# How often the mixer's weight matmuls let other TensorE work in: every 512 contracted rows in place of every 128

## The reference

```python
proj = h @ w_in + b_in                      # 14 groups of columns, the last one 5 x 1024 gates
y_a  = gated delta rule on chunks (l2 norms, triangular solve, scan over the state)
y_b  = causal convolution of 31 taps, layer norm
y_c  = sliding-window attention with sinks, blocks of 128 queries
y_d  = real-gated linear recurrence
y_e  = cross-attention to 256 memory rows
branch_out = einsum('bsnw,nwd->bsnd', [y_a .. y_e], w_br)
merged = sum(sigmoid(gates) * branch_out, axis=branches)
x = x + rms_norm(merged @ w_out)
```

## Time and profile before

| | us |
|---|---|
| three runs | 3691.21, 3688.09, 3692.55 |
| median | 3691.21 |
| the profiled execution | 3682.18 |
| its span, first to last instruction | 3680.3 |

### The profile page before, as it was taken

The page is one execution under the profiler, slowest core; times in us unless marked ns, Lnnn a source line. Parts: engine busy times, 40 slices in busy tenths (PEclk is TensorE's granted clock), DMA queues, the critical chain, the costliest instruction groups (busy, mean ns, idle before and its releaser), DMA issues. The chain is left out here.

```text
span 3680.3 us, 36134 instructions
## 1 busy us (share of the span) xinstructions
PE 3182.3 (86%) x14755; PEld 2462.0 (67%) x14755; DVE 1413.8 (38%) x1628; ACT 1037.5 (28%) x1428; POOL 619.2 (17%) x287
## 2 busy tenths in 40 slices
PE   1976988866499999995599999995999999999995
PEld 1864444425388888884477777774777788888874
DVE  4003333331341414133646777664754122232223
ACT  2113433331211111112246332321333432232222
POOL 1201111012222222220212100001111122222220
PEclk8987999987799999998799999997999999999997
DMA  2213000011011111111223111113333412212121
GB/s 98 91 58 114 18 18 0 1 46 46 19 49 47 51 47 46 51 46 53 105 88 121 52 64 49 50 55 76 114 99 113 177 49 95 92 65 78 52 92 51
DMA packets 105272, 242.61 MB, mean 66 GB/s; under 512 B 7464, under 2 KB 53160, under 8 KB 104872
## 3 DMA queue, kind: packets, MB, share of 16 engines
q1 hardware_dynamic: 96632, 209.65, 16.9%
q10 hardware_dynamic: 8496, 30.94, 2.1%
HBM read 182.89 MB, written 57.67 MB: 65 GB/s over the span
## 5 line engine op out<-in xcount | busy, mean ns | idle before, releaser
L1624 PE MATMUL psum<-normed_hi,w_hi 128*128 128x512 f32 x1632 | 674.7, 413 | 42.6 <-POOL w_lo L2166 37.3
L1626 PE MATMUL psum<-normed_hi,w_lo 128*128 128x512 f32 x1632 | 639.8, 392 | 0.0
L1625 PE MATMUL psum<-normed_lo,w_hi 128*128 128x512 f32 x1632 | 639.1, 392 | 0.0
L2166 POOL TENSOR_TENSOR w_lo<-buffer,w_hi 128x1024 fp32r<-128x1024 f32 x122 | 309.9, 2540 | 1526.5 <-ACT w_hi L1200 1526.5
L1624 PEld LDWEIGHTS psum<-normed_hi,w_hi 128*128 128x128 f32 x1632 | 309.2, 189 | 114.6 <-POOL w_lo L2166 38.8
L1626 PEld LDWEIGHTS psum<-normed_hi,w_lo 128*128 128x128 f32 x1632 | 308.1, 189 | 66.3
L1625 PEld LDWEIGHTS psum<-normed_lo,w_hi 128*128 128x128 f32 x1632 | 309.2, 189 | 63.5 <-issue 7.7
L1200 ACT ACTIVATE buffer<-psum,par 128x512 f32<-128x512 f32 (+1 forms) x196 | 138.0, 705 | 528.2 <-PE psum L1626 513.4
L556 POOL TENSOR_TENSOR w_lo<-buffer,w_hi 128x1024 fp32r<-128x1024 f32 x64 | 156.0, 2438 | 531.6 <-ACT w_hi L590 531.6
L516 PE MATMUL psum<-normed_hi,w_hi 128*128 128x512 f32 x512 | 200.1, 391 | 33.1 <-POOL w_lo L556 33.1
L517 PE MATMUL psum<-normed_lo,w_hi 128*128 128x512 f32 x512 | 199.8, 390 | 0.0
(11 more groups left out here) (318 smaller groups left out, 5320.3 us busy)
## 6 DMA issues: line engine op xcount, KB each, us to landing
buffer<-in_w_in SPq DMA_DIRECT2D x67, 512.0 KB, 4.1
buffer<-in_w_mlp SPq DMA_DIRECT2D x64, 512.0 KB, 3.3
scratch_in<-buffer ACTq DMA_DIRECT2D x59, 512.0 KB, 2.6
buffer<-in_w_gate SPq DMA_DIRECT2D x40, 512.0 KB, 3.4
buffer<-scratch_in SPq DMA_DIRECT2D x32, 512.0 KB, 7.1
buffer<-scratch_y SPq DMA_DIRECT2D x20, 512.0 KB, 7.5
buffer<-in_w_br SPq DMA_DIRECT2D x20, 512.0 KB, 3.3
res<-in_x SPq DMA_DIRECT2D x2, 4096.0 KB, 14.3
```

What stands on the lines that cost most here:

```text
L1624: pe.matmul(out, hi, xh, start=k == 0, stop=False)
L1625: pe.matmul(out, hi, xl, start=False, stop=False)
L1626: mm = pe.matmul(out, lo, xh, start=False, stop=k == unit.kc - 1)
L2166: pool.tensor_tensor(ws.lo[:, n % 2], raw[:, n % 2], ws.hi[:, n % 2].bitcast(F32), ALU.subtract).then_inc(w_lo, 1)
```

## The change

The `gemm` lane on TensorE yields its due time at contraction steps 0 and 4 of a unit only. Four steps (twelve matmuls) in a row can no longer be divided by another lane. A unit of eight steps has two places where other work can enter in place of eight, and a `br` unit one in place of four.

```diff
                     for k in range(unit.kc):
-                        yield pace(n + k / unit.kc)
+                        if k % 4 == 0:
+                            yield pace(n + k / unit.kc)
                         if k == 0:
```

## The result

| | median, us | runs, us |
|---|---|---|
| before | 3689.65 | 3686.48 to 3692.55 |
| changed | 3713.09 | 3710.61 to 3715.89 |

The changed kernel is slower by 23 us, ratio 1.0064 with a 95% interval of 1.0046 to 1.0081. The forecast was 3724 us with a range of 3702 to 3752 us. The profiled execution of the changed kernel took 3714.68 us (span 3712.6 us) and lies close to its median. That of before (3682.18 us) lay 7.5 us under its own: it reached the mixer's first weight matmul at 1792.68 us, the changed one at 1800.94 us, though the program is the same up to there. So the two traces are compared by the length of their stages, not by their spans.

A forecast was written before the change was run, and what follows sets the result against it. In-order TensorE was taken to bound the delta-rule stage, so waits add to the end. Their sums rise from 39.2 to 71.8 us, +32.6 us on the 3691.2 us median: 3724 us, range 3702 to 3752 us.

The forecast's parts named there:

- L1735 to L1742: Delta-rule stage, levels 1 to 5: L1742 directly behind L1735 in 23 levels; TensorE waits 7.5 us before, 22.5 us after.
- L1735 to L1746, level 6: Delta-rule stage: trip of 3.2 us behind ScalarE's exponentials, adjacent in five chunks; waits 9.3 us before, 10.5 us after.
- L1746 and L1725 to the next L1735: Delta-rule stage, two kinds of wait: behind L1746 7.5 us before, 16.8 after; behind L1725 9.0 before, 10.5 after.
- L1704 to L1710: Delta-rule stage: three covering steps gone in three chunks, 1.55 us each; waits 0.8 us before, 4.7 us after.
- L1712 to L1725: Delta-rule stage: one of the two smaller kinds of wait, 4.6 us before and 4.3 us after.
- the first L1692: Delta-rule stage: one of the two smaller kinds of wait, 0.5 us before and 2.5 us after.
- rival c: Delta-rule stage: waits make the clock fall, ten waits of over 2 us cost 20 us, 3744 us; chance 8%.
- rival b: Between delta-rule and window stages: the 41.7 us idle at L1825 swallow the delay, no change, 3691 us; chance 6%.
- rival a: Delta-rule stage: longer batches pay, with fewer changes of work and shrinking trips; faster, about 3680 us; chance 5%.
- Fewer runs: First step behind a small block: each vanished run returns 0.01 us, at the other bound 8 us in all; taken as nothing.
- The window stage: Eight steps between scores and transposes in both orders, so no cost; at most 0.9 us in some eight windows, 7 us.
- The check on the method: Trace of before: waits of some 28 us plus 9 us of matmul tails, together 37 us, against the summed 39.2 us.

## Why the prediction was right, and where its sizes were off

**TensorE is the bound and lost cover is added to the end.** Right. 25.7 of the stage's 27.6 us are idle time of TensorE, and the groups of four in this stage alone reproduce the loss.

**L1735 to L1742.** Right in mechanism and count: 23 adjacent levels, 23 waits. The remainder of time between blocks, taken from the starts in both traces, was 10.3 us at L1742 before and is 21.4 us after (forecast 7.5 and 22.5). Before was sized too small: a block behind even a short wait takes 0.1 us longer (L1742 to L1746 is 2245.31 - 2244.32 = 0.99 us in the earlier trace rows, against 0.89 us), which the formula left out.

**L1735 to L1746, level 6.** All remainders ahead of L1746, with the 0.1 us behind L1742 in the other levels, went from 10.8 to 11.0 us. Of level 6 itself the view of waits shows 6.7 us in both kernels, six waits before and five after; with the tails of the five, 7.5 us stand where 10.5 were forecast. The adjacent trips came to 2.0 to 2.9 us; they too shrank, and only two of the five waits are over 1.5 us.

**L1746 and L1725 to the next L1735.** This is the term that was mis-sized most. Together 18.4 us became 22.4 us, where 16.5 and 27.3 us stood. The trips were taken as fixed, and some are not. Where VectorE had a convolution step or GpSimd's split beside the mask, the trip shrinks when TensorE comes later: L1725 to L1735 in the first chunk is 3.34 us in the changed kernel and was 4.73 us, in the second 4.69 and was 5.60 us, and the 4.3 us behind L1746 in the seventh is 3.4 us. The prediction had 12 us of shrinking trips in its lower bound; here 5 of them came, and 3 in level 6.

**L1704 to L1710, L1712 to L1725, the first L1692.** 0.9 to 5.0, 4.3 to 4.7 and 2.2 to 4.2 us, near the forecast differences (+3.9, -0.3, +2.0).

**The clock (rival c).** The forecast gave it 8% as what decides; it came as a small part. The changed kernel has four stretches in this stage with the clock well under 1.00, before there was one. Two of them, and TensorE in the second:

```profile
2075.00:2090.00 15.00, 10.35 (x53) 9.17 (x53) 9.35 (x11) 1.31 (x3) 0.50 (x1) 0.77 0.28 98
...
2235.00:2245.00 10.00, 8.12 (x46) 7.01 (x45) 7.11 (x13) 2.37 (x6) 0.00 (x0) 0.83 0.01 2
```

```profile
2239.44 0.63 PE L1626 MATMUL psum<-normed_lo,w_hi 128*128 128x512 f32 x1
2239.86 0.63 PE L1627 MATMUL psum<-normed_hi,w_lo 128*128 128x512 f32 x1
...
2242.50 0.40 PE L1625 MATMUL psum<-normed_hi,w_hi 128*128 128x512 f32 x1
```

At 1.2 GHz a 512-column matmul follows the last after 0.42 us in place of 0.23. The four stretches come to 17 us (from the clocks of windows like these), the one before to 3.4 us (2069.6 to 2073.0 us, behind a wait of 2.19 us). What this costs can be read from two pairs of executions in which TensorE's order in the stage is the same. With the eviction moved, no part of the stage ran at 1.2 GHz, and it took 464.3 us against 465.7 us, with the same 29.4 us idle. With groups of four in this stage alone 20.5 us ran at 1.2 GHz, and it took 494.8 us against 493.3 us, with 55.2 and 55.1 us idle. So 3.4 us at 1.2 GHz cost 1.4 to 1.5 us, and the 14 us more of the changed kernel 5 to 6 of its 27.6 us, an estimate from these pairs. The prediction's "no stretch of this stage shows it yet" was a misreading: a mean of 1.00 over 466 us hid the one stretch. Nor does the length of a wait alone decide. The clock fell right behind a wait of 1.88 us at L1747 that ended at 2237.9 us, and did not behind the next one of 1.88 us, nor behind two later ones of 2.3 us at L1736. What decides is open.

**The chain to L1825 (rival b).** 64.8 to 66.9 us in every kernel here, whenever L1786 came. The idle time in the earlier trace rows swallowed nothing.

**Longer batches (rival a).** Undivided units lose 117 us and groups of two lose 6.8 us in the stage; no run shows a net gain by batches as such. A small one is inside the sum: a first step behind a small block, and above all behind one that had waited or has 512 columns, starts late. By the starts these delays came to about 9 us in the stage before and to about 4 us after. The step *Fewer runs* took nothing for this, with 8 us as its other bound.

**The window stage.** The step "cost: nothing" failed: it wins 4.8 us. I counted what TensorE has between scores and transposes, found it the same in both orders, and did not ask what ScalarE's fixed list waits for. A unit's end that comes earlier releases the eviction that stands ahead of the softmax. The forecast of 3724 us is 11 us too high: these 4.8 us, 5 us too many in the delta-rule stage (32.6 for 27.6), and 1.5 us because the median before, 3691.2 us in three executions, is 3689.65 us in four. That the stage was missed by 5 us only is in part luck. With 0.16 us of hidden tail for each of 39 waits before and 55 after, the waits rose by 28 us, not by 32.6. Two terms that the sum took as nothing nearly cancel: the clock adds 5 to 6 us, and fewer late steps give 5 to 6 us back. One step less (0.7 us) makes it the measured 27.6 us.

**Smaller slips.** The check on the method took some 60 waits; the nine kinds of the view are 33, so waits and tails come to 34 us, not 37, while the remainders by the starts come to 47 us: 39.2 us was not confirmed as well as it was said. The longest run of steps before is seven, not twelve. Of the ten waits of over 2 us that rival (c) counted, five came; L1736 waited about 2 us four times, not six.

## What to carry to other kernels

Where one in-order engine carries both a long stream and a latency chain, price each dependent pair as trip less what is issued in between, and look for pairs that a coarser grid makes adjacent; here a chain period of 5.6 and groups of four every 5.8 kept the same pair adjacent for a long time, L1735 and L1742 in 23 of the first 28 levels. Then look at the other engines' fixed lists for waits on the stream's unit ends, since the stream's grain moves those too. The place of the cover matters more than its grain: 33 us were lost with a stream that may be divided at every step and badly placed blocks, and 9 us won in the same stage by moving due times alone.

## What had not been expected

The stages repeat far better than the whole: the delta-rule stage took 465.67, 465.73 and 464.31 us in three kernels that have it in common, 493.25 and 494.77 us in two others, and the differences go with the time at 1.2 GHz; the end from the first L1868 took 847.3 to 849.2 us in all nine, while the mixer's start, behind the same program, came between 1792.7 and 1809.0 us. A change inside a late stage can be read to 1 or 2 us from one trace if its stages are compared.
